# Stationary tiles stored as interleaved high and low words, in a three-pass float32r transformer layer

## The chip, the cores and the metric

The kernel runs on one core of one Trainium2 chip. The metric is device microseconds from the first to the last instruction of one execution; the kernel before takes 2164.75 us, the median of three runs. The engines of a core work side by side: TensorE multiplies (the profile calls it PE, and PEld where it loads the stationary operand of a multiplication), VectorE is DVE, ScalarE is ACT, GpSimd is POOL, and SyncE (SP) issues most transfers.

## The reference

One layer of a hybrid trunk over 2048 latent tokens and 256 context tokens with 1024 features, in float32. Cut to what matters:

```
h  = modulate(rmsnorm(x, norm1_w), m0, m1)         # context tokens likewise
y  = token_mixer(h, hc, w_in, w_out, ...)          # h @ w_in -> conv, gated linear attention, short conv -> @ w_out
x  = x + m2 * y
h  = modulate(rmsnorm(x, norm2_w), m3, m4)
# expert choice: 16 experts take their best 256 tokens each
aff = softmax(h @ router_w); gate, idx = top_k(aff.T, 256)
xs  = h[idx]
hid = silu(xs @ w1[e]) * (xs @ w3[e])              # 1024 x 1024 each
y   = (hid @ w2[e]) * gate ; scatter-add into x
return rmsnorm(x + m5 * y, final_norm_w)
```

## The kernel before

**Three passes for one product.** Every float32 operand of a large product is split into a high part (the value rounded to float32r) and a low part (the remainder). ACT makes the high part by a copy, DVE makes the low part by a subtraction. `mm3` (L53 to L57) then adds three multiplications into one PSUM tile: high by high (L55), high by low (L56), low by high (L57). The first operand of each is the stationary one: it is loaded into the array 128 columns at a time, by a load that the profile shows as LDWEIGHTS on PEld, and the second one, the moving operand, streams through with 256 or 512 columns. Each of the three passes has its own load, also where two passes in a row have the same stationary tile.

**Three places use it.** The input projection keeps `w_in` stationary: `whi` and `wlo`, two buffers each of 8 blocks of 128x128 (L213, L214), written at L533 (ACT) and L711 (DVE), 22 tiles in all; the moving operand is `h_hi`/`h_lo`, 512 latent tokens at a time, or `hc_hi`/`hc_lo`, 256 context tokens. The output projection keeps the mixed tokens stationary: `ct_hi` and `ct_lo` (L1127, L1128), written at L1538 and L1697, 16 tiles; the moving operand is `wo_hi`/`wo_lo`, 512 columns. The experts come last. An expert has 24 items of 1024 words a partition, 16 for `w1` and `w3` in turn and 8 for `w2`. An item is split into `shi` (ACT, L2325) and `slo` (DVE, L2415), which have four buffers. In the first sixteen the items are stationary and the moving operand is `xt_hi`/`xt_lo`, 256 tokens; the result is `bh`. In the last eight the hidden rows `ht_hi`/`ht_lo` are stationary (written at L2333 and L2425, 256 words for each f), and `shi`/`slo` are the moving operand with 512 columns; the result is `eby`. Between them TensorE turns the next expert's tokens (`ebt`, L2267).

**What sets the order.** Each engine has its own list of instructions, written out in the code, and semaphores between them. An item's high part is made when the item four before it has been multiplied (`item_multiplied`), its low part when the high part is there (`w_hi_ready`), and TensorE starts it when the low part is there (`w_lo_ready`). Loops over experts 1 to 14 are loops on the chip; experts 0 and 15 are written out.

Every one of these tiles lies in SBUF with consecutive words of a partition one after another: 128 columns of a block are 512 contiguous bytes, and the high and the low part are separate buffers.

Of the kernel before, what the change touches and what calls it, by code (L numbers as in the profile page):

```python
# [12 lines left out]
F32R = mybir.dt.float32r  # L13
BF16 = mybir.dt.bfloat16
F16 = mybir.dt.float16
I32 = mybir.dt.int32
U32 = mybir.dt.uint32
ALU = mybir.AluOpType
ACT = mybir.ActivationFunctionType
AX = mybir.AxisListType  # L20

P = 128
D = 1024
KD = D // P
# [19 lines left out]
CAP = 256  # L44
# [8 lines left out]
def mm3(nc, out, w_hi, w_lo, x_hi, x_lo, start, stop):  # L53

    nc.tensor.matmul(out, w_hi, x_hi, start=start, stop=False)  # L55
    nc.tensor.matmul(out, w_hi, x_lo, start=False, stop=False)  # L56
    return nc.tensor.matmul(out, w_lo, x_hi, start=False, stop=stop)  # L57
# [37 lines left out]
def phase_project(nc, v, sem, block, low, top, tail):  # L95
# [101 lines left out]
    with ExitStack() as st:  # L197
        sb, _ = alloc(nc, st)
# [11 lines left out]
        one = sb("one", [P, 1])  # L210
        wraw = sb("wraw", [P, KD, P])
        gap = sb("gap", [P, 8])
        whi = [sb(f"whi{i}", [P, KD, P], F32R) for i in range(2)]  # L213
        wlo = [sb(f"wlo{i}", [P, KD, P], F32R) for i in range(2)]  # L214
        stage = [sb(f"stage{i}", [P, NB]) for i in range(NS)]
        v.state = [nc.alloc_sbuf_tensor_at(f"state{g}", [P, NPAIR, DV], F32, offset=top + g * NPAIR * DV * 4)
                   for g in range(HEADS)]
# [877 lines left out]
def tail_stage(nc, v, sem, low, high):  # L1095
# [17 lines left out]
    if True:  # L1113
# [7 lines left out]
        take = area(0, 1)  # L1121
# [2 lines left out]
                        for part, n in enumerate(("wo_hi", "wo_lo")))  # L1124
        raw = [area(1 + i, 1)(f"wo_raw{i}", [P, 4, D]) for i in range(2)]
        take = area(3, 0)
        ct_hi = [take(f"ct_hi{i}", [P, KD, P], F32R) for i in range(2)]  # L1127
        ct_lo = [take(f"ct_lo{i}", [P, KD, P], F32R) for i in range(2)]  # L1128
        take = area(3, 1)
        mb, h2t = take("mb", [P, 3, D]), take("h2t", [P, KD, P])  # L1130
        take, at = place(high + HEADS * (L // P + 2) * DV * 4)
# [640 lines left out]
def route_stage(nc, v, sem, low, high):  # L1772

    SUB = 16
    GE = 8
# [15 lines left out]
    if True:  # L1791
        AREA = KD * NB * 4
        take, at = place(high)
# [14 lines left out]
        take, at = place(v.short_at)  # L1808
        afft, over, thr_wide = take("afft", [P, 2 * P]), take("over", [P, 3, 2 * P], BF16, 2), take("thr_wide", [P, P])
        above, eq, cum_above, cum_eq = (take(n, [P, NE, NT], BF16, 2) for n in ("above", "eq", "cum_above", "cum_eq"))  # L1810
        assert at[0] <= v.short_at + 3 * (NB + 2) * 4
        take, at = place(low + 6 * AREA + 4096 * 1)
        hot_high, hot_low, hot_token = (take(n, [P, 2 * NT, SUB, GE], F16, 2) for n in ("hot_high", "hot_low", "hot_token"))
        slot_above, slot = take("slot_above", [P, NE, NT]), take("slot", [P, NE, NT])
        high16, low16 = take("high16", [P, NT, NE], F16, 2), take("low16", [P, NT, NE], F16, 2)
        found = take("found", [P, 2, SUB, GE], F16, 2)
        assert at[0] <= high
        bgate = [v.bank[5], v.bank[7]]
        bcnt, babove, bthr, beq, btok, bfound = (v.bank[i] for i in (0, 1, 2, 3, 4, 6))
        S = {n: sem("r_" + n) for n in (  # L1820
            "apart_ready", "row_ready", "quarter_ready", "steps_made", "mask8_ready", "scan_set", "steps_set", "lanes_ready",
            "before_ready", "far_ready", "same_ready",
            "aff_turned", "aff_stored", "silu_ready", "bias_loaded", "parts_counted", "counts_summed", "thr_spread", "thr_turned",
            "masks_ready", "scans_ready", "above_ranked", "ties_ranked", "above_read", "hot_low_ready", "low_weighted",
            "tokens_placed", "hot_high_ready", "blocks_ready", "found_ready", "list_ready", "gate_ready",
            "pick_far", "pick_ready", "dve_link")}
# [269 lines left out]
def phase_experts(nc, v, sem, block, start):  # L2096
# [5 lines left out]
    NI, NR = 24, 4  # L2102
    FD = KD
    with ExitStack() as st:
# [3 lines left out]
        def sb(name, shape, dt=F32):  # L2108
            tile = nc.alloc_sbuf_tensor_at(name, shape, dt, offset=at[0])
            at[0] += -(-math.prod(shape[1:]) * 4 // 32) * 32  # L2110
            return tile

        raw, raw_loaded = v.raw, v.s_raw
        shi = [sb(f"shi{i}", [P, D], F32R) for i in range(NR)]
        slo = [sb(f"slo{i}", [P, D], F32R) for i in range(NR)]
        xs = [sb(f"xs{i}", [P, D]) for i in range(2)]
        at[0] += 32
        xt_hi, xt_lo = sb("xt_hi", [P, KD, CAP], F32R), sb("xt_lo", [P, KD, CAP], F32R)
        at[0] += 224
        ht_hi, ht_lo = sb("ht_hi", [P, FD, CAP], F32R), sb("ht_lo", [P, FD, CAP], F32R)  # L2120
        sil = [sb(f"sil{i}", [P, CAP]) for i in range(2)]
        hft = [sb(f"hft{i}", [P, CAP]) for i in range(2)]
        yo = [sb(f"yo{i}", [P, D]) for i in range(2)]
# [7 lines left out]
        bh = [ps(f"bh{i}", [P, 512]) for i in range(2)]  # L2131
# [20 lines left out]
        def item_src(n):  # L2152
            t = raw[item_slot(n)]
            return t[:, :, (n // 2 % 4) * P:(n // 2 % 4 + 1) * P] if n < 16 else t[:, (n - 16) % 4, :]

        def item_dst(buf, n):
            ap = buf[n % NR][:, :]
            return ap.rearrange("p (k c) -> p k c", k=KD) if n < 16 else ap

        def group(t):  # L2160
            return next(g for g, (first, end) in enumerate(ROW_GROUPS) if first <= t < end)
# [15 lines left out]
        if True:  # L2177
# [80 lines left out]
            @block.tensor  # L2258
            def _(pe):
                def turn(e, j):  # L2260

                    s, k0 = j // 2, 4 * (j % 2)
                    pe.wait_ge(S[f"gathered{s}"], e * 16 + 16)
                    if j >= 2:
                        pe.wait_ge(S["x_lo_ready"], e * 4 + (j - 1))
                    for k in range(4):
                        last = nc.tensor.transpose(bt[j % 2][:, k * P:(k + 1) * P],  # L2267
                                                   xs[s][:, (k0 + k) * P:(k0 + k + 1) * P], v.ident[:, :])
                    last.then_inc(S["turned"], 1)

                def down(f, s, half):
                    c, w, n = slice(s * P, (s + 1) * P), slice(half * 512, (half + 1) * 512), 16 + f
                    return mm3(nc, by[2 * s + half][:, :], ht_hi[:, f, c], ht_lo[:, f, c],
                               shi[n % NR][:, w], slo[n % NR][:, w], start=(f == 0), stop=(f == FD - 1))

                def body(e, first, last_e):
                    pe.wait_ge(S["x_lo_ready"], e * 4 + 4)
                    for f in range(FD):
                        wait(pe, S["hidden_ready"], e * FD + (f - 1))
                        for m in range(2):  # L2280
                            n = 2 * f + m
                            pe.wait_ge(S["w_lo_ready"], e * NI + (n + 1))
                            for k in range(KD):
                                c = slice(k * P, (k + 1) * P)
                                last = mm3(nc, bh[f % 2][:, m * CAP:(m + 1) * CAP], shi[n % NR][:, c], slo[n % NR][:, c],
                                           xt_hi[:, k, :], xt_lo[:, k, :], start=(k == 0), stop=(k == KD - 1))
                            last.then_inc(S["item_multiplied"], 1)
                    if not last_e:
                        turn(e + 1, 0)
                        turn(e + 1, 1)  # L2290
                    for f in range(FD - NR if last_e else FD):
                        if f == 2 and not last_e:
                            turn(e + 1, 2)
                            turn(e + 1, 3)
                        n = 16 + f
                        pe.wait_ge(S["w_lo_ready"], e * NI + (n + 1))
                        pe.wait_ge(S["hidden_lo_ready"], e * FD + (f + 1))
                        if f == 0:
                            wait(pe, S["y_ready"], e * 4)
                        for s in range(2):  # L2300
                            for half in range(2):
                                last = down(f, s, half)
                        last.then_inc(S["item_multiplied"], 1)
                    if last_e:
                        for s in range(2):
                            for f in range(FD - NR, FD):
                                if s == 0:
                                    pe.wait_ge(S["w_lo_ready"], e * NI + 16 + f + 1)
                                    pe.wait_ge(S["hidden_lo_ready"], e * FD + (f + 1))
                                for half in range(2):  # L2310
                                    last = down(f, s, half)
                            last.then_inc(S["last_summed"], 1)

                for j in range(4):
                    turn(0, j)
                loop(pe, body)

            @block.scalar
            def _(act):
                def split(e, n):  # L2320
                    key = item_slot(n)
                    if n in (0, 1, 8, 9, 16, 20):
                        act.wait_ge(raw_loaded[key], e * 16 + 16)
                    wait(act, S["item_multiplied"], e * NI + (n - NR + 1))
                    nc.scalar.activation(item_dst(shi, n), item_src(n), ACT.Copy).then_inc(S["w_hi_ready"], 1)  # L2325

                def silu(e, f):
                    act.wait_ge(S["item_multiplied"], e * NI + (2 * f + 2))
# [81 lines left out]
            def _(dve):  # L2410
                link = linker(dve, S["dve_link"])

                def split(e, n):
                    dve.wait_ge(S["w_hi_ready"], e * NI + (n + 1))
                    nc.vector.tensor_tensor(item_dst(slo, n), item_src(n), item_dst(shi, n), ALU.subtract  # L2415
                                            ).then_inc(S["w_lo_ready"], 1)

                def hid(e, f):
# [207 lines left out]
```

## Time and profile before

| | |
|---|---|
| median of 3 runs | 2164.75 us (2163.72 to 2166.89) |
| profiled execution, first to last instruction | 2162.1 us |
| PE / PEld busy | 2063.9 / 1805.6 us |
| DVE / ACT / POOL busy | 1370.5 / 996.3 / 278.0 us |
| mean granted TensorE clock | 0.983 of full |
| HBM traffic | 329.59 MB read, 77.12 MB written |

The profiled execution's own time is its span, 2162.1 us, 2.65 us under the median of the timed runs. A matmul's busy time is not its price: matmuls are pipelined, and each one's record overlaps the next. What one costs in a row of many is the distance from its start to the next one's start, read from a timeline or from a count of them in a stretch. PE and PEld overlap by design. The granted clock is 1.00 (2.4 GHz) in most of the span and 0.5 (1.2 GHz) in a few short pieces.

### The profile page before, as it was taken

Reading aid. Unit: us, or ns where it says so; the run is one execution under the profiler, and the core shown is the slowest. Engines: PE = TensorE matmul, PEld = TensorE weight load, DVE = VectorE, ACT = ScalarE, POOL = GpSimd, SP = SyncE. Lnnn points to the kernel's source line nnn. Section 1 sums busy time; section 2 is a strip of 40 time slices with the busy share of each in tenths; the row PEclk is TensorE's granted clock in tenths of the full one; section 3 lists DMA queues with packets and bytes.
Section 4 is the critical chain, followed back from the end, with each engine's and each line's share of the span. In section 5 each row is a group of like instructions: output and inputs, shape, how many; then the busy total and the mean of one; then the engine's idle time right before and its main releaser. Section 6 shows DMA issues by size and latency. Waiting matters only on the chain.

```text
span 2162.1 us, 34794 instructions
## 1 busy us (share of the span) xinstructions
PE 2063.9 (95%) x13421; PEld 1805.6 (84%) x13421; DVE 1370.5 (63%) x2082; ACT 996.3 (46%) x1630; POOL 278.0 (13%) x357
## 2 busy tenths in 40 slices
PE   6999999999999899994899999999999999999996
PEld 4778888778877677773899999999999999999985
DVE  3664648995994677757555655556565665556557
ACT  5923454344631545532444444445444444444455
POOL 0000000000001011020011112111221112212120
PEclk9999999999999999997899999999999999999998
DMA  7464333333327665456366665576665765657665
GB/s 257 150 241 136 109 106 99 120 114 93 120 90 229 235 204 197 149 197 240 117 213 236 226 218 197 196 251 213 205 215 183 271 209 184 217 206 259 197 225 224
DMA packets 188285, 407.93 MB, mean 189 GB/s; under 512 B 15957, under 2 KB 53397, under 8 KB 187301
## 3 DMA queue, kind: packets, MB, share of 16 engines
q1 hardware_dynamic: 162212, 318.36, 42.7%
q0 software_dynamic: 25984, 88.39, 12.6%
q8 instruction: 56, 0.92, 0.2%
q14 instruction: 33, 0.26, 0.0%
HBM read 329.59 MB, written 77.12 MB: 188 GB/s over the span
## 4 chain that ended last, share of the span: by engine, by line
PE 78%; DVE 11%; DMA 4%; ACT 3%; issue 2%; SPq 2%; POOL 0%; DVEq 0%; ACTq 0%; POOLq 0%
PE bh L55 11%; PE bh L57 11%; PE bh L56 11%; PE bank L55 8%; PE bank L57 8%; PE bank L56 8%; PE eby L55 5%; PE eby L56 5%; PE eby L57 5%; DVE acc L848 4%; PE ebt L2267 1%; DMA wraw<-in_w_in_dram 1%; PE bank L1025 1%; DVE over L2000 1%; PE bank L1407 1%
## 5 line engine op out<-in xcount | busy, mean ns | idle before, releaser
L55 PE MATMUL bh<-xt_hi,shi 128*128 128x256 f32 x2048 | 573.2, 280 | 4.7 <-DVE slo L2415 3.3
L56 PE MATMUL bh<-xt_lo,shi 128*128 128x256 f32 x2048 | 572.7, 280 | 0.0
L57 PE MATMUL bh<-xt_hi,slo 128*128 128x256 f32 x2048 | 572.7, 280 | 0.0
L2415 DVE TENSOR_TENSOR slo<-raw,shi 128x1024 fp32r<-128x1024 f32 x384 | 456.2, 1222 | 157.6 <-ACT shi L2325 153.9
L2325 ACT ACTIVATE shi<-raw 128x1024 fp32r<-128x1024 f32 x384 | 389.8, 1052 | 130.3 <-PE eby L57 127.3
L55 PEld LDWEIGHTS bh<-xt_hi,shi 128*128 128x128 f32 x2048 | 386.8, 189 | 6.0 <-issue 2.0
L56 PEld LDWEIGHTS bh<-xt_lo,shi 128*128 128x128 f32 x2048 | 386.8, 189 | 0.6
L57 PEld LDWEIGHTS bh<-xt_hi,slo 128*128 128x128 f32 x2048 | 386.7, 189 | 0.0
L55 PE MATMUL bank<-h_hi,whi 128*128 128x512 f32 x704 | 282.9, 402 | 1.7 <-DVE wlo L711 1.7
L57 PE MATMUL bank<-h_hi,wlo 128*128 128x512 f32 x704 | 275.2, 391 | 0.0
L56 PE MATMUL bank<-h_lo,whi 128*128 128x512 f32 x704 | 275.0, 391 | 0.0
L55 PE MATMUL eby<-shi,ht_hi 128*128 128x512 f32 x512 | 202.4, 395 | 1.1 <-DVE slo L2415 1.1
L2329 ACT ACTIVATE sil<-bh 128x256 f32<-128x256 f32 x128 | 49.1, 384 | 334.7 <-PE bh L57 334.7
L56 PE MATMUL eby<-slo,ht_hi 128*128 128x512 f32 x512 | 199.6, 390 | 0.0
L57 PE MATMUL eby<-shi,ht_lo 128*128 128x512 f32 x512 | 199.3, 389 | 0.0
L2420 DVE TENSOR_TENSOR hft<-sil,bh 128x256 f32<-128x256 f32 x128 | 53.9, 421 | 190.6 <-ACT sil L2329 190.6
L57 PEld LDWEIGHTS bank<-h_hi,wlo 128*128 128x128 f32 x704 | 132.6, 188 | 28.6
L55 PEld LDWEIGHTS bank<-h_hi,whi 128*128 128x128 f32 x704 | 132.9, 189 | 27.8 <-DVE wlo L711 2.2
L56 PEld LDWEIGHTS bank<-h_lo,whi 128*128 128x128 f32 x704 | 132.9, 189 | 25.7 <-issue 0.5
L2201 POOL TENSOR_TENSOR epause<-epause 128x1 f32<-128x1 f32 x60 | 36.4, 607 | 839.9 <-DVE gidx L2436 469.3
L552 ACT ACTIVATE stage<-bank 128x512 f32<-128x512 f32 (+3 forms) x83 | 47.9, 578 | 188.4 <-PE bank L57 185.4
L848 DVE SCALAR_TENSOR_TENSOR acc<-zbuf,vcol,acc 128x1568 f32<-128x1568 f32 (+14 forms) x60 | 124.9, 2082 | 1.4
(343 smaller groups left out, 3100.6 us busy)
## 6 DMA issues: line engine op xcount, KB each, us to landing
raw<-in_exp_w_dram SPq DMA_DIRECT2D x96, 2048.0 KB, 10.9
uT<-stage POOLq DMA_DIRECT2D x72, 256.0 KB, 2.7
xb<-in_ada_w_dram SPq DMA_DIRECT2D x24, 512.0 KB, 6.0
wraw<-in_w_in_dram SPq DMA_DIRECT2D x22, 512.0 KB, 5.3
adaw<-in_ada_w_dram SPq DMA_DIRECT2D x8, 1024.0 KB, 9.9
xb<-in_x_dram SPq DMA_DIRECT2D x16, 512.0 KB, 4.4
xt<-in_x_dram POOLq DMA_DIRECT2D x16, 512.0 KB, 5.5
x2d<-xt POOLq DMA_DIRECT2D x16, 512.0 KB, 3.1
```

The source lines that it names most:

```text
L55: nc.tensor.matmul(out, w_hi, x_hi, start=start, stop=False)
L56: nc.tensor.matmul(out, w_hi, x_lo, start=False, stop=False)
L57: return nc.tensor.matmul(out, w_lo, x_hi, start=False, stop=stop)
L552: nc.scalar.activation(stage[slot_of[u]][0:m, 0:w], src, ACT.Silu if kind == "r" else ACT.Copy).then_inc(S["act_read"], 1)
L848: nc.vector.scalar_tensor_tensor(a3[:, :, lo:hi], z3[:, :, lo + s:hi + s], wcol, a3[:, :, lo:hi], ALU.mult, ALU.add).then_inc(S["tap_added ...
L1025: nc.tensor.matmul(halves(bk[:, o])[:, :, e, :], (kc if e == early else dm)[half, o], halves(q1[half, o])[:, :, e, :], start=True, stop=True)
L1407: last = nc.tensor.transpose((bi if apart else bt)[:, j * P:(j + 1) * P], h2[t % 2][:, k * P:(k + 1) * P], v.ident[:, :])
L2201: pool.tensor_tensor(pause[:, 1:2], pause[:, 0:1], pause[:, 0:1], ALU.add).then_inc(S["carried"], 1)
L2325: nc.scalar.activation(item_dst(shi, n), item_src(n), ACT.Copy).then_inc(S["w_hi_ready"], 1)
L2329: nc.scalar.activation(sil[f % 2][:, :], bh[f % 2][:, 0:CAP], ACT.Silu).then_inc(S["silu_ready"], 1)
L2415: nc.vector.tensor_tensor(item_dst(slo, n), item_src(n), item_dst(shi, n), ALU.subtract).then_inc(S["w_lo_ready"], 1)
L2420: nc.vector.tensor_tensor(hft[f % 2][:, :], sil[f % 2][:, :], bh[f % 2][:, CAP:2 * CAP], ALU.mult).then_inc(S["hidden_ready"], 1)
```

## The change

High and low parts of a stationary tile share one buffer: word 2i is the high part of element i and word 2i+1 its low part. `whi` and `wlo` become the two halves of `wpair`, `ct_hi` and `ct_lo` those of `ctpair`, `ht_hi` and `ht_lo` those of `htpair`. In the experts the buffers `shi` and `slo` become `split_w`, 2048 words each. Its `w1` and `w3` items are stored interleaved; its `w2` items, which are moving operands, keep each part contiguous in one half of it. So each load of a stationary 128x128 tile reads 128 words that lie 8 bytes apart, and ACT and DVE write these tiles with a step of two words; DVE also reads the high part with that step. Moving operands stay contiguous. Sizes and the addresses of what lies behind the buffers stay as they are, except for one small float16 tile of the routing stage, `found`, which is placed elsewhere.

The instructions on each engine, their order and their waits are the same in both kernels, name by name, apart from the names of the buffers.

```diff
-        whi = [sb(f"whi{i}", [P, KD, P], F32R) for i in range(2)]
-        wlo = [sb(f"wlo{i}", [P, KD, P], F32R) for i in range(2)]
+        wpair = [sb(f"wpair{i}", [P, KD, P, 2], F32R) for i in range(2)]
+        whi, wlo = ([w[:, :, :, half] for w in wpair] for half in range(2))
...
-        ct_hi = [take(f"ct_hi{i}", [P, KD, P], F32R) for i in range(2)]
-        ct_lo = [take(f"ct_lo{i}", [P, KD, P], F32R) for i in range(2)]
+        ctpair = [take(f"ctpair{i}", [P, KD, P, 2], F32R) for i in range(2)]
+        ct_hi, ct_lo = ([c[:, :, :, half] for c in ctpair] for half in range(2))
...
-        shi = [sb(f"shi{i}", [P, D], F32R) for i in range(NR)]
-        slo = [sb(f"slo{i}", [P, D], F32R) for i in range(NR)]
+        split_w = [sb(f"split_w{i}", [P, 2 * D], F32R) for i in range(NR)]
...
-        ht_hi, ht_lo = sb("ht_hi", [P, FD, CAP], F32R), sb("ht_lo", [P, FD, CAP], F32R)
+        htpair = sb("htpair", [P, FD, CAP, 2], F32R)
+        ht_hi, ht_lo = (htpair[:, :, :, half] for half in range(2))
...
-        def item_dst(buf, n):
-            ap = buf[n % NR][:, :]
-            return ap.rearrange("p (k c) -> p k c", k=KD) if n < 16 else ap
+        def item_dst(half, n):
+
+            buf = split_w[n % NR]
+            if n < 16:
+                return buf[:, :].rearrange("p (k c x) -> p k c x", k=KD, x=2)[:, :, :, half]
+            return buf[:, half * D:(half + 1) * D]
```

## Rows read from the trace of the kernel before

**Rows 1.** The page: span, busy time and instructions of the engines.
```profile
span 2162.1 us, 34794 instructions
PE 2063.9 (95%) x13421; PEld 1805.6 (84%) x13421; DVE 1370.5 (63%) x2082; ACT 996.3 (46%) x1630; POOL 278.0 (13%) x357
```

**Rows 2.** The page: the chain that ended last, by engine and by line.
```profile
PE 78%; DVE 11%; DMA 4%; ACT 3%; issue 2%; SPq 2%; POOL 0%; DVEq 0%; ACTq 0%; POOLq 0%
```

**Rows 3.** The page's groups: busy us, mean ns, then idle before and its releaser.
```profile
L55 PE MATMUL bh<-xt_hi,shi 128*128 128x256 f32 x2048 | 573.2, 280 | 4.7 <-DVE slo L2415 3.3
L2415 DVE TENSOR_TENSOR slo<-raw,shi 128x1024 fp32r<-128x1024 f32 x384 | 456.2, 1222 | 157.6 <-ACT shi L2325 153.9
L2325 ACT ACTIVATE shi<-raw 128x1024 fp32r<-128x1024 f32 x384 | 389.8, 1052 | 130.3 <-PE eby L57 127.3
L55 PE MATMUL bank<-h_hi,whi 128*128 128x512 f32 x704 | 282.9, 402 | 1.7 <-DVE wlo L711 1.7
L55 PE MATMUL eby<-shi,ht_hi 128*128 128x512 f32 x512 | 202.4, 395 | 1.1 <-DVE slo L2415 1.1
```

**Rows 4.** Busy time of all engines by stage; the last is the experts.
```profile
core 0: us, PE busy (x) PEld busy (x) DVE busy (x) ACT busy (x) POOL busy (x), PEclk, DMA share, GB/s
40.00:720.00 680.00, 665.11 (x3804) 544.60 (x3805) 474.49 (x758) 321.18 (x615) 54.50 (x100) 0.99 0.42 133
720.00:970.00 250.00, 241.78 (x1309) 189.20 (x1308) 169.97 (x243) 113.69 (x218) 34.73 (x77) 0.99 0.57 199
1040.00:2145.00 1105.00, 1097.56 (x7920) 1034.39 (x7920) 661.81 (x847) 526.87 (x738) 179.18 (x154) 1.00 0.62 215
```

**Rows 5.** The same of `bh` alone, without POOL: first half of experts 1 and 2.
```profile
1111.17:1155.97 44.80, 44.80 (x384) 44.76 (x383) 2.95 (x7) 2.69 (x7) 1.00 0.56 177
1179.56:1224.36 44.80, 44.80 (x384) 44.76 (x383) 2.95 (x7) 2.69 (x7) 1.00 0.55 177
```

**Rows 6.** Timeline of PE, 512-column passes: start us, duration us, instruction.
```profile
1174.80 0.39 PE L55 MATMUL eby<-shi,ht_hi 128*128 128x512 f32 x1
...
1175.94 0.39 PE L57 MATMUL eby<-shi,ht_lo 128*128 128x512 f32 x1
```

**Rows 7.** Timeline of PE, 256-column passes with 32-column stationary tiles.
```profile
52.33 0.28 PE L56 MATMUL bank<-hc_lo,wa_hi 128*32 128x256 f32 x1
52.44 0.28 PE L57 MATMUL bank<-hc_hi,wa_lo 128*32 128x256 f32 x1
```

**Rows 8.** Timeline of PEld, loads between matmuls of one column (x7: seven merged).
```profile
164.12 0.86 PEld L970 LDWEIGHTS bank<-one,xb 128*128 128x128 f32 x7
```

**Rows 9.** PEld groups with loads of 32, 64 and 128 columns.
```profile
L55 PEld LDWEIGHTS bank<-h_hi,wa_hi 128*32 128x32 f32 x32 | 3.5, 109 | 1.4
L55 PEld LDWEIGHTS bank<-h_hi,whi 128*128 128x128 f32 x704 | 132.9, 189 | 27.8 <-DVE wlo L711 2.2 <-issue 0.5
```

**Rows 10.** All engines over that expert (PE, PEld, DVE, ACT, POOL).
```profile
1111.17:1179.56 68.39, 68.39 (x497) 64.53 (x496) 40.57 (x52) 31.95 (x44) 11.89 (x11) 1.00 0.64 216
```

**Rows 11.** Groups of DVE and ACT that write the other stationary tiles.
```profile
L2425 DVE TENSOR_TENSOR ht_lo<-hft,ht_hi 128x256 fp32r<-128x256 f32 x128 | 54.6, 426 | 62.1 <-ACT ht_hi L2333 62.1
L711 DVE TENSOR_TENSOR wlo<-wraw,whi 128x1024 fp32r<-128x1024 f32 x22 | 26.8, 1219 | 29.2 <-ACT whi L533 29.2
L1697 DVE TENSOR_TENSOR ct_lo<-cat,ct_hi 128x1024 fp32r<-128x1024 f32 x16 | 19.6, 1224 | 17.1 <-ACT ct_hi L1538 17.0
```

**Rows 12.** Timeline of DVE in the routing stage: `slot` written in order, then read.
```profile
1017.89 0.42 DVE L2031 TENSOR_TENSOR slot<-bank,slot_above 128x256 f32<-128x256 f32 x1 [0.56 <-PE bank L1940]
...
1018.75 0.58 DVE L2034 SCALAR_TENSOR_TENSOR low<-slot,high 128x256 f16<-128x256 f32 x1
```

**Rows 13.** The chain in order of time, 385 to 400 us.
```profile
387.44 2.05 DVE acc L848
389.50 1.13 DVE wlo L711
390.63 2.01 DVE acc L848
```

More of the change, by code:

```diff
@@ L1810, in route_stage @@
         above, eq, cum_above, cum_eq = (take(n, [P, NE, NT], BF16, 2) for n in ("above", "eq", "cum_above", "cum_eq"))
+        found = take("found", [P, 2, SUB, GE], F16, 2)
         assert at[0] <= v.short_at + 3 * (NB + 2) * 4
@@ L1815, in route_stage @@
         high16, low16 = take("high16", [P, NT, NE], F16, 2), take("low16", [P, NT, NE], F16, 2)
-        found = take("found", [P, 2, SUB, GE], F16, 2)
         assert at[0] <= high
@@ L2273, in down @@
                     return mm3(nc, by[2 * s + half][:, :], ht_hi[:, f, c], ht_lo[:, f, c],
-                               shi[n % NR][:, w], slo[n % NR][:, w], start=(f == 0), stop=(f == FD - 1))
+                               item_dst(0, n)[:, w], item_dst(1, n)[:, w], start=(f == 0), stop=(f == FD - 1))
                 def body(e, first, last_e):
@@ L2283, in body @@
                             for k in range(KD):
-                                c = slice(k * P, (k + 1) * P)
-                                last = mm3(nc, bh[f % 2][:, m * CAP:(m + 1) * CAP], shi[n % NR][:, c], slo[n % NR][:, c],
+                                last = mm3(nc, bh[f % 2][:, m * CAP:(m + 1) * CAP], item_dst(0, n)[:, k, :], item_dst(1, n)[:, k, :],
                                            xt_hi[:, k, :], xt_lo[:, k, :], start=(k == 0), stop=(k == KD - 1))
@@ L2324, in split @@
                     wait(act, S["item_multiplied"], e * NI + (n - NR + 1))
-                    nc.scalar.activation(item_dst(shi, n), item_src(n), ACT.Copy).then_inc(S["w_hi_ready"], 1)
+                    nc.scalar.activation(item_dst(0, n), item_src(n), ACT.Copy).then_inc(S["w_hi_ready"], 1)
                 def silu(e, f):
@@ L2414, in split @@
                     dve.wait_ge(S["w_hi_ready"], e * NI + (n + 1))
-                    nc.vector.tensor_tensor(item_dst(slo, n), item_src(n), item_dst(shi, n), ALU.subtract
+                    nc.vector.tensor_tensor(item_dst(1, n), item_src(n), item_dst(0, n), ALU.subtract
                                             ).then_inc(S["w_lo_ready"], 1)
```

## The prediction

> **What bounds the kernel now.** I read the page first. TensorE is busy for 95% of the span, and its loads for 84% [rows 1]. The chain that ended last is 78% TensorE and 11% DVE [rows 2]. TensorE hardly waits for the tiles that the change touches: over the whole kernel its first passes wait 4.7 us in `bh`, 1.7 us in the input projection and 1.1 us in `eby` [rows 3]. By stage, the experts take 1105 of the 2162.1 us, with TensorE busy for 1097.56 us [rows 4]. Expert 1 alone shows PE busy without a gap, 68.39 of 68.39 us [rows 10]. So half of the time is a stream of three-pass products at TensorE's own pace, and the other large stages are near it.
>
> The pace is what the change can touch. In the first half of an expert 384 passes of 256 columns take 44.80 us, that is 116.7 ns from one start to the next, the same in two experts, at a granted clock of 1.00 (2.4 GHz) [rows 5]. Passes of 512 columns start 228 ns apart: 1.14 us for five of them [rows 6]. The 256 further columns cost 111 ns, 0.435 ns each, against 0.417 ns for one cycle at 2.4 GHz; some 5 ns a pass do not depend on the columns.
>
> Is 116.7 ns the pace of the stream or of the load? Each pass has a load of 128 columns. Two rows speak to it. Where the matmul has a single column and hides nothing, seven loads take 0.86 us; less the last one's own record of 0.19 us [rows 9], six distances make 0.67 us, 111 ns each [rows 8]. That is what a contiguous load of 128 columns needs. And with stationary tiles of only 32 columns, whose load record is 109 ns long instead of 189 [rows 9], 256-column passes still start 110 to 120 ns apart (52.33 to 52.44 us) [rows 7]. So the stream sets the pace, and the load stands just inside it: 111 of 116.7 ns, with 5 to 6 ns of room. The 512-column passes leave 117 ns.
>
> **The change part by part.** Nothing is added, removed or reordered, so every term is a duration that a stride of two words may alter.
>
> *Loads in the first half of the experts.* 16 experts of 384 make 6144 [rows 3, 5]. The price is the load's time above 116.7 ns. No load here has a stride, so it is bounded by neighbours. From below: a load that got no longer, or shorter, gives 0, since the stream sets the pace. For the cheap end the rows hold a measure: the record of a load grows by 80 ns for 96 columns (189 less 109) [rows 9], 0.83 ns a column, so a contiguous load passes over 4 bytes in 0.83 ns. With the stride it must pass over 8 bytes in that time, 9.6 bytes a nanosecond. The moving operand passes over 4 bytes in 0.42 to 0.435 ns [rows 5, 6], 9.2 to 9.6 bytes a nanosecond, all the time. SBUF delivers that rate to this engine already, so I take 0. From above: if a load took twice 111 ns, the pace would be 222 ns, and 6144 times 105 is 647 us.
>
> Here the Trainium skill bears on it. Advanced Engine Details and Errata, "SBUF Cachelines", says that SBUF is read in lines of 16 bytes and that at least two accesses must fall into one line for full speed. Four-byte words 8 bytes apart make exactly two, so by this rule the load stays at full speed, with nothing to spare; by it the sum stays at zero. No row of this case has a strided load, so the trace can't confirm it.
>
> *Loads elsewhere.* 704, 256 and 512 groups of three passes with 512 columns have 117 ns of room, so even a doubled load (222 of 228 ns) is hidden: 0. The 144 passes on 256 context tokens are in the position of `bh`; doubled they cost 15 us, otherwise 0.
>
> *DVE and ACT in the experts.* 256 items with 1222 ns on DVE and 1052 ns on ACT [rows 3], and 128 hidden tiles of 256 words with 426 ns on DVE [rows 11]. The nearest row for a strided access: DVE writes 256 words of `slot` in order in 0.42 us, and an instruction of the same size, also with two inputs, that reads them 16 words apart takes 0.58 us [rows 12], 0.63 ns a word more. A step of two words is far nearer to the contiguous one, so I take no change; the upper bound is 0.65 us for 1024 words. It would be hidden too. An item is multiplied in 24 times 116.7, 2.8 us. DVE would need 1.87 us for its split and some 0.5 us for its half share of the two hidden-tile instructions, together 2.4. Over an expert DVE is busy for 40.57 of 68.39 us [rows 10]; 16 times 0.65 and 8 times 0.16 make 52.3. The latency from freed buffer to low part grows from 2.3 to 3.6 us, and there are three items, 8.4 us, ahead. Cost 0. What hides it is the four buffers.
>
> *DVE and ACT elsewhere.* 22 tiles of the input projection at 1219 ns and 16 of the output projection at 1224 ns on DVE [rows 11]. Here DVE is busy for 474.49 of 680 us [rows 4] and in places is itself the path: at 389.50 us `wlo` stands in the chain between two convolution steps [rows 13]. At the upper bound 22 times 0.65 is 14 us, if each were on the path, plus 1.3 us for the first `ct` tile. I take 0, bound 15.
>
> *`found`* is a placement only: 0.
>
> **Sum.** 0 on the profiled execution's 2162.1 us, which is 2.7 us under the median of the runs. The forecast is the median unchanged: 2164.75, rounded to 2165 us. A change of less than 0.2%, 4.3 us, can't be told from none here.
>
> **The rivals.**
>
> *A, the strided load is slower and becomes the bound of the experts (slower).* The place is the first half of each expert, the price 6144 times what a load needs beyond 116.7 ns. It decides from a load only 5% longer than today's 111 ns; each further percent is 6.8 us. A quarter more (139 ns) makes 136 us, 2300 us in all; half more makes 306 us, 2471 us; twice makes 2812 us, or 2827 us with the context passes. For it: the room is tiny, and nothing here shows such a load. Against it: the moving operand is read over as many bytes in a nanosecond. The load records would lengthen from 189 ns, or start 120 ns apart and more.
>
> *B, strided writes slow DVE and ACT (slower, small).* Hidden in the experts as above; 5 to 15 us from the input projection where DVE is the path, 2170 to 2180 us. The expert pace would stay at 116.7 ns and L711 and L2415 would show more than 1222 ns.
>
> *C, the stream gets faster.* A pass takes 10 ns more than its 106.7 ns of columns at 2.4 GHz, and 15 ns more with 512 columns. If loads and stream hinder each other at the memory and the new layout removes it, 6144 times up to 10 and 4416 times up to 15 ns make 128 us: 2037 us; half of it 2101, a quarter 2133. Against it: the pass with a 32-column load has the same distance [rows 7], so a load four times as short does not help the stream. The Trainium skill, TensorE: Matmul & The Clock Gate, "Step-by-step: what each phase is for", says that the two operands have independent read ports; by that C gives nothing, and the row agrees.
>
> *D, loads and stream hinder each other more than before.* Interleaved loads touch twice the span of memory. Each nanosecond over all 10,560 passes costs 10.6 us; at 3 ns, 2197 us. The same row speaks against it.
>
> **How the numbers follow.** No measurable change 0.54. A 0.15, B 0.10, D 0.08, C 0.13. This gives faster 0.13, same 0.54, slower 0.33. The predicted time is the likeliest case, 2165 us, whose own range is 2160 to 2170. For eight in ten the range takes in B, D, a load up to some 23% longer, and the quieter third of C: 2125 to 2290. Outside are most of A (0.11) and most of C (0.08).
>
> **What would show it.** The `bh` stretch of expert 1 at 384 passes in 44.8 us shows that the load stayed inside the stream; a longer one is A or D, told apart by the 512-column passes, which A leaves at 228 ns and D does not. The records at L533, L711, L2325 and L2415 at 1.05 and 1.22 us show the writes free; above 1.3 us is B. A `bh` pace under 116 ns is C. The forecast is wrong if the load's rate with a step of two words falls by more than the 5% that the stream leaves.

## The result and the profile after

The changed kernel takes 2205.11 us (median of four runs, 2201.74 to 2210.03), the kernel before 2165.82 us beside it: 1.0182 times as long, 95% interval 1.0168 to 1.0196. The forecast was no measurable change, under 4.3 us either way; the time rose by 39.3 us, and lies inside the stated range.

The page of the changed kernel, its span, its engines and its chain, against [rows 1, 2]:

```profile
span 2208.2 us, 34794 instructions
PE 2110.5 (96%) x13421; PEld 1852.9 (84%) x13421; DVE 1371.1 (62%) x2082; ACT 1024.5 (46%) x1630; POOL 281.1 (13%) x357
PE 82%; DVE 9%; ACT 3%; issue 2%; DMA 2%; SPq 1%; POOL 0%; DVEq 0%; ACTq 0%; POOLq 0%
```

The span grew by 46.1 us, PE's busy time by 46.6 us. That is more than the 39.3 us of the medians, because the profiled execution of the changed kernel is the slowest of its four (2210.03 us) and that of the kernel before the fastest (2163.72 us). DVE is unchanged and ACT has 28 us more. The groups, against [rows 3, 9, 11]:

```profile
L55 PE MATMUL bh<-xt_hi,split_w 128*128 128x256 f32 x2048 | 584.9, 286 | 2.1 <-DVE xt_lo L2433 1.4
L2417 DVE TENSOR_TENSOR split_w<-raw,split_w 128x1024 fp32r<-128x1024 f32 x384 | 456.4, 1223 | 168.8 <-ACT split_w L2327 164.2
L2327 ACT ACTIVATE split_w<-raw 128x1024 fp32r<-128x1024 f32 x384 | 413.8, 1118 | 134.3 <-PE eby L57 127.9
L55 PEld LDWEIGHTS bh<-xt_hi,split_w 128*128 128x128 f32 x2048 | 402.4, 197 | 3.5 <-DVE xt_lo L2433 1.8
L55 PE MATMUL bank<-h_hi,wpair 128*128 128x512 f32 x704 | 287.3, 408 | 0.0
```

TensorE waits no longer than before for these tiles, DVE's subtractions kept their 1.22 us, and a strided load's record is 8 ns longer, 197 for 189. The pace tells more. Instructions of `bh` alone over the first halves of experts 1 and 2, same columns as [rows 5]:

```profile
1133.87:1179.94 46.07, 46.07 (x384) 46.03 (x383) 2.95 (x7) 2.70 (x7) 1.00 0.55 172
1204.10:1250.17 46.07, 46.07 (x384) 46.03 (x383) 2.95 (x7) 2.70 (x7) 1.00 0.54 171
```

384 passes take 46.07 instead of 44.80 us: 120.0 ns each instead of 116.7, at the same clock of 1.00. The 512-column passes, against [rows 6]:

```profile
1199.20 0.39 PE L55 MATMUL eby<-split_w,htpair 128*128 128x512 f32 x1
...
1200.36 0.39 PE L57 MATMUL eby<-split_w,htpair 128*128 128x512 f32 x1
```

Five distances make 1.16 us. Taken over whole groups of three passes, the median distance is 233.3 ns in the input projection and `eby` and 235.3 ns in the output projection; it was 226.7 ns in all three. So the pass whose load has some 110 ns of room lost twice as much as the one whose load has 5. The passes on the 256 context tokens are the exception: their stationary tiles are interleaved too, and their median stayed at 120.0 ns. By stage: the first pass of the output projection and the first of `bh`, in the timelines of the kernel before and then of the changed one:

```profile
733.63 0.79 PE L55 MATMUL bank<-wo_hi,ct_hi 128*128 128x512 f32 x1 [6.24 <-DVE ct_lo L1697]
1040.60 0.58 PE L55 MATMUL bh<-xt_hi,shi 128*128 128x256 f32 x1 [1.41 <-DVE xt_lo L2431]
```

```profile
745.00 0.80 PE L55 MATMUL bank<-wo_hi,ctpair 128*128 128x512 f32 x1 [6.62 <-DVE ctpair L1697]
1061.39 0.58 PE L55 MATMUL bh<-xt_hi,split_w 128*128 128x256 f32 x1 [1.41 <-DVE xt_lo L2433]
```

The input projection is 11.4 us longer, the part from there to the experts 9.4 us, and the experts take the other 25.3 us. An expert from its first pass to the next one's, all engines, against [rows 10]:

```profile
1133.87:1204.10 70.23, 70.23 (x498) 66.32 (x497) 40.60 (x52) 33.47 (x44) 12.13 (x11) 1.00 0.61 211
```

It is 1.84 us longer, 1.27 of it in `bh`, with PE busy throughout. (Sixteen times that is 29 us, not 25.3: in the kernel before, TensorE waited 3.3 us for DVE in the last expert.) Over the whole kernel the mean distance grew by 3.1 ns for 6144 passes and by 6.2 ns for 4416, together 46 us, which is what the span grew by. So the loss is a slower pace of the passes with a strided stationary tile, the context passes excepted; single stages differ from it by a few us of waits and of low clock.

### The profile page after: what moved, and what is told of

Read it like the earlier page. It is cut to its first block, busy times and chain, and to the rows that moved or that the text cites. A ratio compares the mean times of both kernels' runs of the same rounds, so it can differ in the third digit from the quotient of the medians.

```text
span 2208.2 us, 34794 instructions
## 1 busy us (share of the span) xinstructions
PE 2110.5 (96%) x13421; PEld 1852.9 (84%) x13421; DVE 1371.1 (62%) x2082; ACT 1024.5 (46%) x1630; POOL 281.1 (13%) x357
## 4 chain that ended last, share of the span: by engine, by line
PE 82%; DVE 9%; ACT 3%; issue 2%; DMA 2%; SPq 1%; POOL 0%; DVEq 0%; ACTq 0%; POOLq 0%
PE bh L55 11%; PE bh L56 11%; PE bh L57 11%; PE bank L55 9%; PE bank L57 9%; PE bank L56 9%; PE eby L55 5%; PE eby L57 5%; PE eby L56 5%; DVE acc L848 3%; PE ebt L2270 1%; PE bank L1025 1%; DVE over L2000 1%; PE bank L1407 1%; PE bank L1004 1%
## 5 line engine op out<-in xcount | busy, mean ns | idle before, releaser
L55 PE MATMUL bh<-xt_hi,split_w 128*128 128x256 f32 x2048 | 584.9, 286 | 2.1 <-DVE xt_lo L2433 1.4
L56 PE MATMUL bh<-xt_lo,split_w 128*128 128x256 f32 x2048 | 584.6, 285 | 0.0
L57 PE MATMUL bh<-xt_hi,split_w 128*128 128x256 f32 x2048 | 584.5, 285 | 0.0
L2417 DVE TENSOR_TENSOR split_w<-raw,split_w 128x1024 fp32r<-128x1024 f32 x384 | 456.4, 1223 | 168.8 <-ACT split_w L2327 164.2
L2327 ACT ACTIVATE split_w<-raw 128x1024 fp32r<-128x1024 f32 x384 | 413.8, 1118 | 134.3 <-PE eby L57 127.9
L55 PEld LDWEIGHTS bh<-xt_hi,split_w 128*128 128x128 f32 x2048 | 402.4, 197 | 3.5 <-DVE xt_lo L2433 1.8
L56 PEld LDWEIGHTS bh<-xt_lo,split_w 128*128 128x128 f32 x2048 | 402.4, 197 | 0.6
L57 PEld LDWEIGHTS bh<-xt_hi,split_w 128*128 128x128 f32 x2048 | 402.4, 196 | 0.0
L55 PE MATMUL bank<-h_hi,wpair 128*128 128x512 f32 x704 | 287.3, 408 | 0.0
L57 PE MATMUL bank<-h_hi,wpair 128*128 128x512 f32 x704 | 279.0, 396 | 0.0
L56 PE MATMUL bank<-h_lo,wpair 128*128 128x512 f32 x704 | 278.8, 396 | 0.0
L55 PE MATMUL eby<-split_w,htpair 128*128 128x512 f32 x512 | 204.8, 400 | 0.9 <-DVE split_w L2417 0.9
L57 PE MATMUL eby<-split_w,htpair 128*128 128x512 f32 x512 | 201.7, 394 | 0.0
L56 PE MATMUL eby<-split_w,htpair 128*128 128x512 f32 x512 | 201.7, 394 | 0.0
L57 PEld LDWEIGHTS bank<-h_hi,wpair 128*128 128x128 f32 x704 | 137.3, 195 | 28.8
L55 PEld LDWEIGHTS bank<-h_hi,wpair 128*128 128x128 f32 x704 | 138.0, 196 | 25.3 <-issue 0.5
L56 PEld LDWEIGHTS bank<-h_lo,wpair 128*128 128x128 f32 x704 | 137.5, 195 | 25.1 <-issue 0.5
```

What stands on the lines that cost most here:

```text
L2327: nc.scalar.activation(item_dst(0, n), item_src(n), ACT.Copy).then_inc(S["w_hi_ready"], 1)
L2417: nc.vector.tensor_tensor(item_dst(1, n), item_src(n), item_dst(0, n), ALU.subtract).then_inc(S["w_lo_ready"], 1)
```

## The experiments

Each run's time stands beside the kernel before on the same chip (2165.4 to 2166.3 us). Where there is one run, the paces of its trace carry the reading.

**Where the cost is.** In the first kernel only the `w1` and `w3` items are interleaved, in the second everything but them.

```diff
 # bh_only: whi, wlo, ct_hi, ct_lo, ht_hi, ht_lo as before; split_w as in the change
 # no_bh: the changed kernel with
-                return buf[:, :].rearrange("p (k c x) -> p k c x", k=KD, x=2)[:, :, :, half]
+                return buf[:, half * D:(half + 1) * D].rearrange("p (k c) -> p k c", k=KD)
```

> Only the w1 and w3 items of the experts are interleaved (the stationary tiles of bh); whi/wlo, ct and ht lie as before. If each place pays for its own strided loads: bh 120.0 ns, input and output projection and eby as before (226.7 ns), and 6144 times 3.33 ns, 20.5 us over before, 2186 us. If the strided writes of ACT in the experts were what holds TensorE up, eby would be slower too.

> The changed kernel with the w1 and w3 items contiguous again: input projection, output projection and eby have strided loads, bh has none; found stays at its new place. bh back at 116.7 ns, the 512-column passes at 233.3 ns; the rest of the change's cost, some 21 us over before, 2187 us. With the run that interleaves bh alone it adds up to the changed kernel's 2205 us, to 2 us.

2182.32 us (1.0079, 1.0062 to 1.0096) and 2186.56 us (1.0095, 1.0079 to 1.0112): 16.5 and 20.7 us over before, together 37.2 of the 39.3 us. Again `bh` alone in expert 2, of the first and of the second:

```profile
1183.86:1229.93 46.07, 46.07 (x384) 46.03 (x383) 2.95 (x7) 2.68 (x7) 1.00 0.54 174
```

```profile
1198.12:1242.92 44.80, 44.80 (x384) 44.76 (x383) 2.96 (x7) 2.70 (x7) 1.00 0.54 172
```

Each place pays for its own loads: 120.0 ns and 116.7 ns in `bh`, while the 512-column passes stay at 226.7 ns in the first and at 233.3 ns in the second. The strided writes are not what holds TensorE up: in the second kernel the experts' only strided writes are those of `htpair`, 14 of whose 16 an expert fall into `bh`, and `bh` keeps its 116.7 ns; `eby`, beside which the other two fall, has 233.3 ns throughout. The second kernel keeps the moved `found`, and its `bh` runs as before.

**Which pass pays.** Only one part of each tile is strided, made of two tiles that share a buffer. In the experts two items then share it, so ACT waits for one item more before it writes an even one; PE stays busy throughout all the same. The kernel of step 4 below has the same extra wait.

```diff
-        wlo = [sb(f"wlo{i}", [P, KD, P], F32R) for i in range(2)]
+        lopair = sb("lopair", [P, KD, P, 2], F32R)
+        wlo = [lopair[:, :, :, i] for i in range(2)]
...
-        ct_hi = [take(f"ct_hi{i}", [P, KD, P], F32R) for i in range(2)]
+        hipair = take("hipair", [P, KD, P, 2], F32R)
+        ct_hi = [hipair[:, :, :, i] for i in range(2)]
...
+            buf = slopair[n % NR // 2]     # items 2j and 2j+1 share it; shi stays contiguous
+                return buf[:, :].rearrange("p (k c x) -> p k c x", k=KD, x=2)[:, :, :, n % 2]
```

> Only one of the two parts of each stationary tile is read with a step of two words, in the same memory as before: in the input projection the low parts of two tiles share a buffer, in the output projection the high parts of two tiles, in bh the low parts of two items; ht stays contiguous. Theory M (the reads of a strided load hold up the stream under which they run): each load runs beside the pass ahead of it, so only that pass gets longer. bh: the distance from the pass of L56 to that of L57 is 120 ns, the other two 116.7 ns; input projection 233.3 ns from L56 to L57 and 226.7 ns otherwise; output projection (high parts strided, loads of L55 and L56): from L57 to L55 and from L55 to L56 233.3 ns, from L56 to L57 226.7 ns; eby 226.7 ns throughout. Theory W (TensorE is paced by how much it does, whatever pass does it): all three distances rise alike by a third, bh 117.8 ns, input projection 228.9 ns, output projection 231.1 ns. In both the sum is about a third of 46 us over before: 2176 to 2184 us.

2184.07 us. Expert 2's `bh` takes 45.65 us for its 384 passes:

```profile
1189.12:1234.77 45.65, 45.65 (x384) 45.61 (x383) 2.95 (x7) 2.69 (x7) 1.00 0.56 187
```

That is 118.9 ns, two thirds of the loss from a third of the strided loads. In experts 1 to 13, which have no waits in `bh`, the mean distances within a triple are 116.9 ns from L55 to L56, 120.4 from L56 to L57 and 119.4 from L57 to L55 (before, 116.7 each). Here the pass beside the strided load got longest, and the one behind it got longer too. The projections don't repeat that. In the input projection the medians are 231, 230 and 232 ns (before, 227 each), all alike, though only the load of L57 is strided. In the output projection, where the loads of L55 and L56 are, they are 227, 231 and 235 ns: the distance that theory M left alone grew, and one that it made longer did not. `eby`, all contiguous, kept 226.7 ns. So neither theory holds: a strided load's cost is not confined to the pass beside it, and costs don't add up load by load.

**Is it TensorE's own activity?** Zeros in place of `w1` and `w3`, the experts' output being left out by it.

```diff
-                    nc.scalar.activation(item_dst(0, n), item_src(n), ACT.Copy)
+                    nc.scalar.activation(item_dst(0, n), item_src(n), ACT.Copy, scale=0.0 if n < 16 else 1.0)
...
-  item_src(n), item_dst(0, n), ALU.subtract
+  item_src(n), item_dst(0, n), ALU.mult if n < 16 else ALU.subtract
```

> The changed kernel, whose w1 and w3 items are multiplied by zero where they are split, so that bh's stationary tiles and with them ht are all zeros (the experts add nothing to the output). Layout, instructions and waits are those of the changed kernel. Theory M (reads of SBUF): bh stays at 120.0 ns and eby at 233.3 ns. Theory W (TensorE is held back by its own activity, as data make it): bh falls to 107 to 113 ns, eby to 214 to 220 ns.

2208.05 us, and the pace is the same to the nanosecond, so the data are not the cause, and theory W falls in the form in which they matter:

```profile
1201.67:1247.74 46.07, 46.07 (x384) 46.03 (x383) 2.95 (x7) 2.70 (x7) 1.00 0.54 171
```

**How steep is the step?** Step 4 everywhere, then step 3 in the input projection and step 8 in the output projection.

```diff
-        wpair = [sb(f"wpair{i}", [P, KD, P, 2], F32R) for i in range(2)]
+        wquad = sb("wquad", [P, KD, P, 4], F32R)
+        whi, wlo = ([wquad[:, :, :, 2 * i + half] for i in range(2)] for half in range(2))
 # ctquad, htquad and the split_w buffers of four parts alike; in step3_8, on the kernel before:
+        wtriple, wlast = sb("wtriple", [P, KD, P, 3], F32R), sb("wlast", [P, KD, P], F32R)
+        ctwide = [take(f"ctwide{i}", [P, P, KD], F32R) for i in range(4)]
```

> Four stationary tiles share a buffer word by word, in the same memory: every load reads words 16 bytes apart, in all four places. Theory M with lines of 16 bytes: the load touches 128 lines, where the changed kernel touches 64 and the kernel before 32, so three times the extra reads: bh 126.7 ns, 512-column passes 246.7 ns, some 2300 us. Theory L (a load by itself reads a line in a fixed time, and has now become the bound): the pace is the load's own, near 220 ns for bh and unchanged or little above 233 ns for 512 columns, load records near 300 ns, some 2800 us. Theory W (step of two costs, whatever the step): bh 120.0 and 512 columns 233.3 ns, 2205 us.

> Two other steps, experts as before. Input projection: three of the four stationary tiles interleaved (step 3 words, 12 bytes), the fourth contiguous. Output projection: the blocks of a tile interleaved (step 8 words, 32 bytes). If a load takes the larger of 107 ns and 1.67 ns per 16-byte line it touches (32, 64, 96, 128 lines for steps 1 to 4, never more than 128), less a common start of some 80 ns: load records 188 ns contiguous, 240 to 250 ns at step 3, 310 ns at step 8, the same as at step 4, and the 512-column passes stay between 230 and 240 ns. If the distance in bytes counts and not the line, step 8 has records near 500 ns and output-projection passes above 400 ns.

At step 4 the kernel takes 2944.05 us. Expert 2's `bh`:

```profile
1325.85:1415.33 89.48, 89.48 (x384) 89.44 (x384) 2.94 (x7) 2.69 (x7) 1.00 0.35 114
```

The groups of loads of that kernel:

```profile
L55 PEld LDWEIGHTS bh<-xt_hi,split_w 128*128 128x128 f32 x2048 | 673.6, 329 | 1.8 <-DVE xt_lo L2435 1.8
L55 PEld LDWEIGHTS bank<-h_hi,wquad 128*128 128x128 f32 x704 | 218.1, 310 | 3.7 <-DVE wquad L711 2.6
```

The load has become the bound, as theory L had it: 233 ns a pass, twice 116.7, while the median of the 512-column passes is 236 ns. Theory M, with a price for each line that a load touches, had 246.7 ns there; from step 2 to step 4 the lines double, and the pass got only some 3 ns longer. The groups of the other kernel (2201.99 us): loads of step 3, contiguous, and step 8; then the writes of ACT and DVE, step 3 and step 8.

```profile
L56 PEld LDWEIGHTS bank<-h_lo,wtriple 128*128 128x128 f32 x704 | 178.5, 253 | 0.5 <-issue 0.4
L57 PEld LDWEIGHTS bank<-h_hi,wlast 128*128 128x128 f32 x352 | 66.2, 188 | 0.1
L56 PEld LDWEIGHTS bank<-wo_lo,ctwide 128*128 128x128 f32 x256 | 84.5, 330 | 1.6
L534 ACT ACTIVATE wtriple<-wraw 128x1024 fp32r<-128x1024 f32 x22 | 35.3, 1604 | 5.0 <-DMA wraw<-in_w_in_dram 4.9
L712 DVE TENSOR_TENSOR wtriple<-wraw,wtriple 128x1024 fp32r<-128x1024 f32 x11 | 17.1, 1555 | 21.4 <-ACT wtriple L534 21.4
L1698 DVE TENSOR_TENSOR ctwide<-cat,ctwide 128x1024 fp32r<-128x1024 f32 x16 | 34.2, 2137 | 31.8 <-ACT ctwide L1539 31.8
```

Load records are 188, 196, 253, 310 to 329 and 330 ns at steps 1, 2, 3, 4 and 8. By the 0.83 ns a column of [rows 9], 128 columns are 107 of the 188 ns; less the other 81 ns the records are 107, 115, 172, 229 to 248 and 249 ns: nearly flat to step 2, then steep to step 4, and hardly further. That is in step with the lines of 16 bytes touched, 96 at step 3 and 128 at steps 4 and 8. The Trainium skill, Advanced Engine Details and Errata, "SBUF Cachelines" (full speed needs two accesses to a line), is borne out for the load by itself: step 2 is the last before the cliff.

The passes tell where that matters. In the second of these kernels the 512-column passes, whose loads have room, have a median of 235.7 ns at step 3 in the input projection (where all three loads are strided) and of 245.7 ns at step 8 in the output projection, the latter above the 230 to 240 ns expected. The context passes, with 256 columns and next to no room, have 175.7 ns at step 3, and 233.3 ns at step 4 in the first kernel.

**Does the address matter?** First the distance between stationary and moving tiles in the changed kernel, then in the one before.

```diff
 # offset_after, of the changed kernel; offset_before, of the kernel before, has += 288 and no `gap` (32 bytes ahead of whi)
-        at[0] += 32
         xt_hi, xt_lo = sb("xt_hi", [P, KD, CAP], F32R), sb("xt_lo", [P, KD, CAP], F32R)
-        at[0] += 224
+        at[0] += 256
```

> The changed kernel with xt_hi and xt_lo 32 bytes lower, all else at its place: the distance between the addresses of the stationary and the moving tiles of bh is 0 instead of 32 bytes beyond a multiple of 1024. Theory A (load and stream now run through the memory at the same rate of bytes and collide at this distance): bh moves off 120.0 ns by at least 3 ns, eby stays at 233.3 ns. Theories M and W: bh stays at 120.0 ns, 2205 us.

> The kernel before with other distances between stationary and moving tiles, modulo 64 bytes: bh 0 instead of 32, input projection and eby 32 instead of 0; all contiguous. If the address distance matters for contiguous loads (bh's 116.7 ns against the 120 ns of the context passes suggests it): bh 120.0 ns, and the input projection and eby below 226.7 ns, perhaps 223.3 ns; the sum 20 us less 3648 times 3.3 ns, about 2173 us. If it doesn't: all paces and 2165 us unchanged.

The changed kernel doesn't notice this shift: 2205.94 us, `bh` at 120.0 ns. The kernel before does notice its own: 2198.34 us (1.0150, 1.0133 to 1.0167), the same instructions and all tiles contiguous. Its `bh` in expert 2:

```profile
1193.60:1239.67 46.07, 46.07 (x384) 46.02 (x383) 2.95 (x7) 2.69 (x7) 1.00 0.53 172
```

120.0 ns, the pace of the interleaved tiles; and the input projection and `eby` went from 226.7 to 233.3 ns, their other pace too. The output projection, whose tiles did not move, kept 226.7 ns. My hope of a gain with 512 columns was wrong in sign. A gain did come in the context passes, which the expectation doesn't price. The first and the last of 24 in a row, in the kernel before and then with the tiles moved:

```profile
254.57 0.28 PE L55 MATMUL bank<-hc_hi,whi 128*128 128x256 f32 x1
...
257.32 0.28 PE L57 MATMUL bank<-hc_hi,wlo 128*128 128x256 f32 x1
```

```profile
257.59 0.28 PE L55 MATMUL bank<-hc_hi,whi 128*128 128x256 f32 x1
...
260.27 0.28 PE L57 MATMUL bank<-hc_hi,wlo 128*128 128x256 f32 x1
```

23 distances make 2.75 and 2.68 us, 120 and 117 ns. In three places, then, a shift by 32 bytes moves contiguous tiles between the two paces that the change moved them between. Interleaving cost nothing in the one place where the kernel before already had the slower pace.

In the input projection and in `eby` only the stationary tiles moved, and their loads did not get slower. The loads of `eby` before and after the move:

```profile
L57 PEld LDWEIGHTS eby<-shi,ht_lo 128*128 128x128 f32 x512 | 96.2, 188 | 20.4
L57 PEld LDWEIGHTS eby<-shi,ht_lo 128*128 128x128 f32 x512 | 96.2, 188 | 23.3
```

So where a load reads slows the stream beside it, even though that load is as quick as before and has some 110 ns to spare. This is the nearest that the runs come to showing the mechanism.

Then sweeps, the four buffers of the experts at four places each, and a placement made from one of them.

```diff
+        PITCH = D + 4          # 2 * D + 4 in sweep_after, D + 8 in sweep32_before
+        sweep = sb("sweep", [P, 2 * NR * PITCH], F32R)
+        shi = [sweep[:, i * PITCH:i * PITCH + D] for i in range(NR)]
 # tuned_after, of the changed kernel:
+        xt_both = sb("xt_both", [P, 4 + 2 * KD * CAP + 4], F32R)     # xt_hi starts 16 bytes in
```

> The kernel before; each of the four shi and slo buffers of the experts starts 16 bytes further than the last, beyond the multiple of 64 bytes at which they lay. The distance from the stationary to the moving tile, modulo 64 bytes, is then 32, 16, 0, 48 for the items n mod 4 = 0, 1, 2, 3 of bh, and 0, 48, 32, 16 for f mod 4 of eby (where shi and slo are the moving operand). Theory C (load and stream run beside each other through one memory, and their distance decides): bh items at distance 32 have 116.7 ns, at 0 120.0 ns, those at 16 and 48 something else; eby 226.7 ns at 0, 233.3 ns at 32. If one of the untried distances is free of collisions it lies below the best so far, bh near 113 ns or eby near 220 ns. If the distance is not what decided, but the order of the buffers in memory: all items alike.

> The same sweep in the changed kernel: the four split_w buffers start 16 bytes further each, so that bh's distances are 32, 16, 0, 48 modulo 64 for n mod 4 and eby's 0, 48, 32, 16 for f mod 4. Theory C, in the form that an interleaved load has no good distance: bh 120.0 ns for all four kinds of item and eby 233.3 ns for all. In the form that it has one, not yet tried: one kind of item at 116.7 ns or below, and the change could be had without loss by placing the tiles.

> The kernel before; the four shi and slo buffers start 0, 32, 64 and 96 bytes beyond a multiple of 128, shi and slo of an item alike. bh's distance from stationary to moving tile is then 32, 0, 96, 64 bytes modulo 128 for n mod 4 = 0, 1, 2, 3, eby's 0, 96, 64, 32 for f mod 4. Theory C with a period of 64 bytes: bh 116.7 ns at 32 and 96, 120.0 ns at 0 and 64; eby 226.7 ns at 0 and 64, 233.3 ns at 32 and 96. With a period of 128 bytes or more: 96 and 64 differ from 32 and 0. A pace under 116.7 or 226.7 ns anywhere would give a placement better than the kernel before's.

> The changed kernel with xt_hi and xt_lo 16 bytes higher, so that every item of bh has the distance 48 bytes, at which the items n mod 4 = 3 of the sweep ran at 118.6 ns. Theory C: bh 118.6 ns throughout, 6144 times 1.4 ns less, 8.6 us, so 2197 us; all else as in the changed kernel. If the place of the buffer and not the distance made that item faster: 120.0 ns and 2205 us.

Mean paces of `bh` in experts 1 to 14, from the second pass of an item to its last, for n mod 4 = 0, 1, 2, 3: contiguous with 16 bytes between, 118.6, 119.6, 119.0, 118.3 ns (2181.18 us); contiguous with 32 bytes, 119.0, 119.3, 118.1, 115.0 ns (2179.11 us); interleaved with 16 bytes, 120.0, 122.2, 120.1, 118.6 ns (2207.48 us). `eby`, read the same way, had 230.0 to 232.8 ns in the contiguous ones, 232.4 to 233.3 ns in the interleaved. In the sweep by 32 bytes, from the second to the last pass of item 5 and then of item 7:

```profile
1476.03 0.28 PE L56 MATMUL bh<-xt_lo,sweep 128*128 128x256 f32 x1
...
1478.65 0.28 PE L57 MATMUL bh<-xt_hi,sweep 128*128 128x256 f32 x1
...
1481.72 0.28 PE L56 MATMUL bh<-xt_lo,sweep 128*128 128x256 f32 x1
...
1484.24 0.28 PE L57 MATMUL bh<-xt_hi,sweep 128*128 128x256 f32 x1
```

22 distances make 2.62 and 2.52 us, 119 and 115 ns, for the same work. Place decides, but not by the rule I gave: items at a distance of 32 bytes ran at 118.6 and 119.0 ns instead of 116.7. The placed kernel settles it: at the distance where the sweep had 118.6 ns it ran `bh` at 120.0 ns,

```profile
1197.77:1243.84 46.07, 46.06 (x384) 46.03 (x383) 2.95 (x7) 2.70 (x7) 1.00 0.53 171
```

and took 2204.73 us (1.0182, 1.0165 to 1.0199), the changed kernel's time. Theory C in the form of one distance modulo 64 or 128 bytes falls. One more rival falls with the sweeps: that at step 2 the load itself needs 120 ns and has become the bound of `bh`. Interleaved items of n mod 4 = 3 ran at 118.6 ns, and 512-column passes slowed with room to spare. That load and stream hinder each other is the reading that fits all runs; that they do so at the memory is argued, which addresses collide is open, and so is why a 512-column pass loses 6.7 ns and one of 256 columns 3.3 ns. No version was run that beats the kernel before; the 115 ns of one kind of item says that one may exist.

## Why the prediction was wrong

*The pace belongs to the stream, the load stands inside it.* Right for the kernel before. At step 4 the load did become the bound. At step 2 it did not, and the stream's own pace rose, also where the load had some 110 ns of room. (The 228 ns read from [rows 6] are 226.7 ns over many passes, so the part of a pass that does not depend on its columns is nearer to 10 ns than to the 5 ns given first.)

*Loads at no cost.* This is the step that failed: "SBUF delivers that rate to this engine already, so I take 0." The rate argument was about one reader. It is right for that reader: the load's record grew only from 188 to 196 ns. But the sum also needed that a load which stays hidden costs the stream nothing, and that was put at nothing without a row for it. The stream lost 3.3 ns on 256 columns. Nor is the rate what costs: contiguous loads, at half the bytes a nanosecond, cost the same 3.3 ns from another address. I took a test of speed for a test of independence.

*512-column passes at no cost, as hidden.* It failed with it, and it is the larger half: 20.7 us of no_bh against 16.5 of bh_only. Room for the load is not cover for the stream.

*Rival D* was the likeliest mechanism, with a chance of 0.08 and a guess of 3 ns on all passes, 2197 us. Measured: 3.3 and 6.7 ns in undisturbed rows; the means over all 6144 and 4416 passes grew by 3.1 and 6.2 ns, 46 us in the trace, and the medians of the runs differ by 39. That 2205 us lies inside the stated range is owed to rivals A and B, which widened it and did not come. I held the 32-column row against it [rows 7]; it shows that a short load has the same pace, not that a differently placed or spaced one has. The sentence of the Trainium skill (TensorE: Matmul & The Clock Gate, "Step-by-step: what each phase is for") that the two operands have independent ports spoke the same way. These runs contradict it, if it is read as no interference: moving only the stationary tiles of the input projection by 32 bytes took its passes from 226.7 to 233.3 ns.

*Rival A* was wrong below step 3 and right above. *Rival B*: ACT is slower, DVE not, and the experts hide it as worked out: L2327 with 1118 for 1052 ns on average. *Rival C* did not come. `found` cost nothing.

## What to carry to other kernels

In this kernel a step of two float32 words in a stationary tile cost its float32r passes some 3% against a well-placed contiguous tile, and nothing against a badly placed one. A larger step ruins the passes whose load has no room (256 columns: 176 ns at step 3, 233 at step 4), and far less those whose load has it (512 columns: 236 ns at both). That an operand's load is hidden says nothing of what it does to the stream beside it: price an edit of its layout on every pass, not on those where the load is nearly the bound. And when a layout changes, compare with the same layout at another address first.

## What was unexpected of the hardware

- Moving contiguous tiles by 32 bytes made the kernel before 1.5% slower (2198.34 us) with the same instructions; one placement ran a quarter of the `bh` items at 115.0 ns, below the 116.7 ns of the kernel before.
- Writes: 1024 words take DVE 1.22 us at steps 1 and 2, 1.56 at 3 and 2.14 at 8; ACT 1.05 us at step 1 and 1.60 at 3.
- Stationary tiles of nothing but zeros left the pace at 120.0 ns exactly.
- The same 32 bytes that slowed `bh` from 116.7 to 120.0 ns took the context passes from 120.0 to 116.7 ns.
